# A mixture-of-experts stage with its experts ranked on the chip: fullest by twos, the others by fours

## The reference, cut to what matters

```python
p_group = softmax(t @ wg + bg); p_top_g, g_idx = top_k(p_group, 1)
e_logits = take_along_axis(einsum('td,gde->tge', t, we) + be, g_idx)[:, 0]
p_top_e, e_idx = top_k(softmax(e_logits), 2)
w_sel = p_top_g * p_top_e / sum(p_top_e)
combine = w_sel placed at (group, expert), zero elsewhere
for gi in range(4):
    hid = silu(t @ w_gate[gi]) * (t @ w_up[gi]) * combine[:, gi]     # per expert
    out = out + hid @ w_down[gi]
```

## Time and profile before

| | |
|---|---|
| profiled execution's own time | 1947.95 us |
| its span, first to last instruction | 1946.2 us |
| TensorE matmul busy | 1761.8 us (91%) |
| VectorE / ScalarE busy | 504.7 / 319.5 us |
| read from HBM | 348.36 MB, 180 GB/s over the span |
| mean granted TensorE clock | 0.942 of 2.4 GHz |

### The profile page before, as it was taken

One profiled execution on the slowest core, in us unless ns is written; L12 is line 12 of the kernel. 1 busy time (PEld: TensorE's weight loads), 2 busy tenths in 40 slices (PEclk: granted clock), 3 DMA queues, 4 the chain that ended last, 5 costly groups with the idle time before them and its releaser, 6 DMA issues.

```text
span 1946.2 us, 20288 instructions
## 1 busy us (share of the span) xinstructions
PE 1761.8 (91%) x8574; PEld 1020.0 (52%) x8574; DVE 504.7 (26%) x1222; ACT 319.5 (16%) x656; POOL 0.2 (0%) x4
## 2 busy tenths in 40 slices
PE   5899679999699999999988999997889998979797
PEld 2555578788644444444433444443664443457565
DVE  2200453412211011111014620204661013040481
ACT  2210220110200000000003200011231110031271
POOL 0000000000000000000000000000000000000000
PEclk9899866999899999999998999999899999979898
DMA  9667900323669999999981212221001111122100
GB/s 365 253 244 283 379 13 1 130 90 144 266 252 425 428 425 427 426 428 427 426 347 36 87 44 87 87 87 43 1 1 43 68 62 57 73 76 104 46 2 22
DMA packets 31953, 350.48 MB, mean 180 GB/s; under 512 B 3879, under 2 KB 10184, under 8 KB 11016
## 3 DMA queue, kind: packets, MB, share of 16 engines
q1 hardware_dynamic: 26448, 341.85, 43.3%
q10 hardware_dynamic: 5432, 7.58, 1.1%
HBM read 348.36 MB, written 1.05 MB: 180 GB/s over the span
## 4 chain that ended last, share of the span: by engine, by line
PE 81%; DVE 9%; ACT 4%; issue 2%; DMA 2%; PEld 1%; PEldq 0%; ACTq 0%; DVEq 0%; SPq 0%
PE bank L644 29%; PE bank L1310 11%; PE bank L1355 6%; PE bank L673 4%; PE bank L1300 3%; PE bank L1986 3%; PE bank L1320 3%; PE bank L661 2%; PE bank L1981 2%; PE bank L502 2%; PE bank L1074 1%; PE bank L1062 1%; PE bank L824 1%; PE bank L815 1%; PE bank L1865 1%
## 5 line engine op out<-in xcount | busy, mean ns | idle before, releaser
L644 PE MATMUL bank<-H,ring 128*128 128x512 f32 (+1 forms) x1632 | 551.8, 500 | 16.5 <-DVEq L285 8.2
L644 PEld LDWEIGHTS bank<-H,ring 128*128 128x128 f32 x1632 | 314.4, 194 | 247.7 <-issue 215.0
L1310 PE MATMUL bank<-ring,work 128*64 128x512 f32 x768 | 226.1, 593 | 0.8 <-DVE work L1397 0.8
L1310 PEld LDWEIGHTS bank<-ring,work 128*64 128x64 f32 x768 | 77.5, 137 | 142.4 <-issue 141.4
L1355 PE MATMUL bank<-work 128*64 128x512 f32 x512 | 113.4, 594 | 8.0 <-DVE work L1397 7.6
L1310 PE MATMUL bank<-work 128*64 128x512 f32 x256 | 113.2, 595 | 0.0
L673 PE MATMUL bank<-ring,H 128*128 128x512 f32 x192 | 83.6, 594 | 0.0
L1418 DVE TENSOR_TENSOR work<-work,bank 128x512 f32<-128x512 f32 x16 | 11.0, 689 | 266.0 <-PE bank L1310 266.0
L1355 PEld LDWEIGHTS bank<-work 128*64 128x64 f32 x512 | 41.9, 137 | 69.2 <-issue 57.8
L1300 PEld LDWEIGHTS bank<-work 128*128 128x128 f32 x512 | 60.2, 196 | 15.3 <-issue 12.2
L1300 PE MATMUL bank<-work 128*128 128x128 f32 x512 | 63.2, 283 | 2.9 <-DVE work L1405 2.9
(11 more groups left out here) (351 smaller groups left out, 1748.4 us busy)
## 6 DMA issues: line engine op xcount, KB each, us to landing
ring<-in_moe_w_gate SPq DMA_DIRECT2D x32, 2048.0 KB, 13.0
work<-in_moe_w_down SPq DMA_DIRECT2D x32, 2048.0 KB, 13.4
ring<-in_moe_w_up SPq DMA_DIRECT2D x16, 2048.0 KB, 11.5
work<-in_moe_w_up SPq DMA_DIRECT2D x16, 2048.0 KB, 16.0
ring<-in_ab_w_in SPq DMA_DIRECT2D x14, 2048.0 KB, 8.0
ring<-in_ada_w SPq DMA_DIRECT2D x12, 2048.0 KB, 9.7
ring<-in_w_in SPq DMA_DIRECT2D x12, 2048.0 KB, 8.2
ring<-in_w_mod SPq DMA_DIRECT2D x12, 2048.0 KB, 9.0
```

The source lines that it names most:

```text
L644: mm = nc.tensor.matmul(bank[i % NB][:, 0:n], weight(c, k, j * P, (j + 1) * P), rhs(k), start=(k == 0), stop=(k == kt - 1))
L1310: mm = nc.tensor.matmul(bank[b][rows, :], x[:, k, rows], pair_slot[i + e][:, k * 512:(k + 1) * 512], start=(k == 0), stop=(k == DT - 1), s ...
```

## The change

The router also ranks the experts by token count on the chip. After the place matmuls, VectorE forms a key for each expert (32 x count - number) in a row, TensorE transposes it, VectorE counts the greater keys (`rank`) and makes a permutation matrix (`ranked`); six small matmuls bring `place`, the combine weights, the experts' numbers (`ids`) and the keys into ranked order. The overflow test now asks whether the fullest has more than 64 tokens or the ninth more than 32.

The expert stage takes the 24 less full experts first, by fours with 32 slots each in 6 passes, and then the eight fullest by twos with 64 slots in 4 passes, all written out without run-time loops. SyncE waits for `ids_out`, reads the experts' numbers into registers, and loads half matrices of 1 MB (8 KB per partition, out of rows of 16 KB) into eight slots of 1 MB: six in the ring, two in `work`. A step is one half of gate, up or down for all experts of the pass; TensorE reports each with `step_used`, and a load waits until the step that used its slot eight pieces ago is done. Nothing is loaded for the experts before the ranking is there. Two of the three ring slots come free for the second block with the last hidden product, the third after the last down step.

```diff
-CAP = 64
+N_WIDE = 8
+CAP_WIDE, CAP_SLIM = 64, 32
+CAP = CAP_WIDE
...
-            slot_until[s] = (now[0] + i, "experts")
+            slot_until[s] = (now[0] + i, "experts" if i < 2 else "experts' last")
...
+            pe.wait_ge(lane_out, 1)
+            nc.tensor.transpose(bank[0][0:2 * NX, 0:P], key_row, ident[:])
+            for t in range(TT):
+                mm = nc.tensor.transpose(bank[1][0:2 * NX, t * P:(t + 1) * P], by_expert[:, t, :], ident[:])
+            mm.then_inc(lane_mm, 1)
+            pe.wait_ge(lane_out, 2)
+            for t in range(TT):
+                for half in range(2):
+                    rows = slice(half * NX, (half + 1) * NX)
+                    nc.tensor.matmul(bank[6 + half][:, t * NX:(t + 1) * NX], by_lane[rows, t * P:(t + 1) * P], ranked[rows, :],
+                                     start=True, stop=True, skip_group_check=True)
+            nc.tensor.matmul(bank[6][:, 4 * NX:5 * NX], bc(vec("lane")[0:NX, :], [NX, P]), ranked[0:NX, :], start=True, stop=True, skip_group_check=True)
+            nc.tensor.matmul(bank[6][:, 5 * NX:6 * NX], bc(key_col[0:NX, :], [NX, P]), ranked[0:NX, :],
+                             start=True, stop=True, skip_group_check=True).then_inc(lane_mm, 1)
...
+            L(V.tensor_tensor(by_expert[:, :, 0:NX], bank[0][:, 0:2 * NX].rearrange("p (t e) -> p t e", e=NX), member, ALU.mult))
+            L(V.tensor_copy(by_expert[:, :, NX:2 * NX], comb))
+
+            L(V.scalar_tensor_tensor(out=key_row[:, 0:NX], in0=bank[1][:, 0:NX], scalar=float(NX), in1=slot_no[:, 0:NX], op0=ALU.mult, op1=ALU.subtract))
+            V.tensor_copy(key_row[:, NX:2 * NX], key_row[:, 0:NX]).then_inc(lane_out, 1)
+            dve.wait_ge(lane_mm, 1)
+            both = slice(0, 2 * NX)
+            L(V.tensor_copy(key_col[both, :], bank[0][both, 0:1]))
+            L(V.tensor_scalar(above[both, :], key_row[both, 0:NX], key_col[both, :], None, ALU.is_gt))
+            L(V.tensor_reduce(rank[both, :], above[both, :], AXX, ALU.add))
+            L(V.tensor_copy(by_lane[both, :], bank[1][both, 0:T]))
+            V.tensor_scalar(ranked[both, :], slot_no[both, 0:NX], rank[both, :], None, ALU.is_equal).then_inc(lane_out, 1)
+            dve.wait_ge(lane_mm, 2)
+            L(V.tensor_copy(ids, bank[6][:, 4 * NX:5 * NX]))
...
+            V.tensor_tensor(over, last_col[:, 0:1], last_col[:, 1:2], ALU.max).then_inc(ids_out, 1)
+            L(V.tensor_scalar(place.rearrange("p t e -> p (t e)"), bank[6][:, 0:2 * NX], -1.0, None, ALU.add))
+            L(V.tensor_copy(comb_s.rearrange("p t e -> p (t e)"), bank[7][:, 0:2 * NX]))
...
+        PASSES = [(N_WIDE + 4 * i, 4) for i in range((NX - N_WIDE) // 4)] + [(2 * i, 2) for i in range(N_WIDE // 2)]
+        HALF = SLOT // 2
+        NHALF = 8
...
+        def half_src(w, e, half):
+
+            return w[bass.ds(e, 1), :, half * HALF:(half + 1) * HALF].rearrange("e p n -> p (e n)")
+
+        def sparse_sync(sp):
+            for p, (first, experts) in enumerate(PASSES):
+                e = [sp.value_load(ids[0:1, first + i:first + i + 1], min_val=0, max_val=NX - 1) for i in range(experts)]
+                for j, w in enumerate((wg, wu, wd)):
+                    for half in range(2):
+                        n = 6 * p + 2 * j + half
+                        for i in range(experts):
+                            at = load_at[n] + i
+                            if at >= NHALF:
+                                sp.wait_ge(step_used, step_of[at - NHALF] + 1)
+                            sp.dma_start(half_slot[at % NHALF], half_src(w, e[i], half)).then_inc(step_in[n % 4], 16)
...
         def moe_sync(sp):
-            pair_loads(sp, 0, True)
-            sp.wait_ge(stage_done, 3 * 6)
+            sp.wait_ge(ids_out, 1)
+            sp.wait_ge(stage_done, 3 * 5)
...
+            def project(p, b, n):
+
+                experts = PASSES[p][1]
+                w = P // experts
+                for half in range(2):
+                    pe.wait_ge(step_in[(n + half) % 4], filled_to[n + half])
+                    for k in range(4 * half, 4 * half + 4):
+                        for e in range(experts):
+                            rows = slice(e * w, (e + 1) * w)
+                            mm = nc.tensor.matmul(bank[b][rows, :], gath[:, k, rows], half_slot[(load_at[n + half] + e) % NHALF][:, (k % 4) * 512:(k % 4 + 1) * 512],
+                                                  start=(k == 0), stop=(k == DT - 1), skip_group_check=True)
+                    mm.then_inc(step_used, 1)
...
+            last_use["experts' last"] = (moe_ring_free, 2)
```

More of the change, by code:

```diff
@@ L1111, in build @@
         hrows = ar.take(TT, D)
-        place = ar.take(TT, NX + 2)
+        place = ar.take(TT, NX)
+        comb_s = ar.take(TT, NX)
+        ids = ar.take(NX).bitcast(I32)
         slot_no = ar.take(CAP)
@@ L1320, in scatter @@
                         mm = nc.tensor.matmul(bank[4 + 2 * t + half][:], pick_t[:, t, :], py[:, half * 512:(half + 1) * 512],
-                                              start=start, stop=stop, skip_group_check=True)
+                                              start=(p == 0), stop=(p == NPASS - 1), skip_group_check=True)
                 return mm
[L1324 to L1336, removed]
+            gather(0)
+            for p in range(NPASS):
+                pe.wait_ge(gath_out, 2 * p + 2)
+                project(p, 0, 6 * p)
+                if p:
+                    scatter(p - 1)
+                project(p, 1, 6 * p + 2)
+                if p < NPASS - 1:
+                    gather(p + 1)
                 pe.wait_ge(hid_out, p + 1)
@@ L1344, in pair @@
                 mm.then_inc(pick_mm, 1)
-                if not last:
-                    pe.wait_ge(gath_out, p * 2 + 4)
+                if p < NPASS - 1:
+                    pe.wait_ge(gath_out, 2 * p + 4)
                 pe.wait_ge(phid_t_out, p + 1)
[L1348 to L1366, removed]
+                down(p, 6 * p + 4)
+            scatter(NPASS - 1).then_inc(scat_mm, 1)
         def sparse_act(act):
-            def take_gathered(n):
-                act.wait_ge(gath_mm, n)
+            def take_gathered(p):
+                act.wait_ge(gath_mm, 2 * p + 1)
@@ L1408, in make_pick_w @@
             def make_pick_w(p):
-                for t in range(TT):
-                    for e in range(2):
-                        ins = nc.vector.tensor_scalar(pick_w[:, t, e * CAP:(e + 1) * CAP], slot_no, of(place, t, p * 2 + e),
-                                                      of(comb, t, p * 2 + e), ALU.is_equal, ALU.mult)
-                ins.then_inc(pick_w_ready, 1)
-            def pair(p, last):
-                dve.wait_ge(up_mm, p + 1)
+                o, shape, first, experts, w = slots(p, pick_w)
```

150 lines of the change are left out of this document (78 added, 72 removed).

## The result

The changed kernel takes 1977.44 us in the median of 4 runs, the kernel before 1950.68 (4 runs on the same chip): ratio 1.014, interval [1.0116, 1.0164], 27 us slower. The forecast was 1968, and the sign and most of the terms came as written, but the sum of the terms was +16.9 us and the measured change is 10 us more. The profiled execution took 1976.9 us.

The account below looks back on a forecast made before the run. The prediction took TensorE, closely followed by the 201.3 MB weight transfer, to bound the expert stage. Ranking and reads (first issue 546.8), stream (to 1025.9) and tail (8.1) gave +16.9 us, a forecast of 1968 us, range 1956 to 1993.

Parts of the forecast that it names:

- The bound: Expert stage: TensorE paces it with the DMA queue also full; with TensorE's work cut, the 201.3 MB transfer stands behind it.
- Four experts side by side: Expert projections: one over four 32-column tiles takes about 7 us, like one over two 64-column tiles (6.87).
- The chain in front: Router's end: ranking gives the identities at 543.8 us, register reads follow, first weight issue at 546.8.
- The register reads: SyncE before the first load: overflow flag, branch and four identities take 3.0 us, bounds 1.2 and 5.9.
- The stream: Expert weight loads: all 201.3 MB follow the first issue, 476 us (bounds 471 and 510) plus 3.1 around them.
- The price of 8 KB rows: Half-matrix loads: 423 GB/s, from a line through 427 with 16 KB rows and 395 with 1.7 KB packets.
- The ring starves: Rival, chance 0.10: in passes by fours eight slots hold only two steps; late returns cost 40 us, total 2008.
- The limit of 7.5 us: Passes by fours: TensorE must return a step within some 7.5 us of its landing; half clock needs 6.9 to 7.0.
- The tail: After the last landing: last down half 3.55, hand-over 0.89 and scatter 3.68, together 8.1 us, ending at 1034.0.
- No slower: Rival, chance 0.10: 426 GB/s is TensorE's demand, not the queue's limit; at 438 the sum is zero, at 448 total 1942.
- The sum: Whole stage: its end moves from 1017.14 to 1034.0 us, +16.9; +10 with the low ends, +54 with the high.
- the two slower rivals: Dearer half matrices (chance 0.14; 1984 at 410 GB/s, 2002 at 395) and the starving ring (0.10; 2008).

Follow-up runs that it names:

- e8: The changed kernel, eight slots kept, with useless matmuls filling TensorE's idle time in the passes by fours; stage 503.0 us, ratio 1.0120 to the kernel before.
- e1: The changed kernel with 14 slots of 1 MB instead of 8, nothing else; stage 501.5 us, ratio 1.0115 to the kernel before.
- e7: The kernel before with the first pair's early loads held back until the router stage ends; stage 489.8 us against 480.1, ratio 1.0053.
- e6: Changed kernel with experts 0 to 3 fixed first, 28 ranked, and seven 2 MB slots with whole matrices; stage 476.6 us, ratio 0.9993 to the kernel before.
- e5: Changed kernel with experts 0 to 3 fixed first by twos, 28 ranked, and 14 slots of 1 MB; stage 476.2 us, ratio 0.9975 to the kernel before.

## Why the prediction was right or wrong

**The bound.** Right. TensorE's work fell out of the way in the passes by fours, and the stage became the transfer of 201.3 MB plus what stands in front of and behind it.

**Four experts side by side.** Right: a half step takes 3.64 us at full clock; by twos a whole projection takes 7.09, so a half 3.55.

**The chain in front.** Right in its sum. The identities stood 5.96 us after the place product (539.91 and 0.16), 6.7 by the forecast. The register reads came to 3.3 us up to the first issue, 3.0 forecast; in the chain the flag takes 0.9 with the branch, and each identity 0.54 to 0.58 from one read to the next. First issue: 9.3 us behind the place product, 9.7 forecast. The 3.0 was a choice between bounds of 1.2 and 5.9 with no row for a single read, so its closeness is in part luck. The six small matmuls took 1.9 us where 2.7 stood.

**The stream.** Here the sum failed. From the first issue to the landing of the last piece I had 479.1 us (3.1 + 476). The last piece landed at 1034.9: 491.5 us, 12.4 too long. The price of 8 KB rows explains 2 to 3: 420 to 421 GB/s instead of 423, close to the line drawn through 16 KB and 1.7 KB. The other 9 are the rate in the passes by fours, 361 x (1 - 410/421) = 9.4 us.

**The rival that was real.** "The ring starves" was priced as all or nothing: 40 us if the clock stayed down during dense work, one to two us otherwise. The clock did come back in dense work, as expected, and 9 us were lost all the same. Two things in that step were wrong. The limit of 7.5 us for returning a step was worked out as if the queue gave its full rate until it is empty; steps returned after 5.9 to 6.4 us, inside the limit, and around 620 and 680 us the rate had already fallen to 384 to 393, with the share at 0.97 to 0.99. It is no fixed line either: between 550 and 590 us steps came back after 6.0 to 6.2 us, and the rate held at 417 to 422. And I counted the half clock as harmless because a whole step at half clock would still fit, so its only price seemed to be the one late down step. e8 shows that the late return by the clock causes the loss with this ring, and e1 that a deeper ring takes it away with the clock still low (0.81); so it takes both, a cold engine and a shallow ring.

**The tail.** Right. 1043.30 - 1034.9 = 8.4 us, 8.1 forecast.

**No slower.** Its condition, a queue that reaches 438 GB/s when asked, is refuted: 420 to 421 in e1 over 361 us with work always queued, 425 to 430 in whole 2 MB loads in e7, and 427 in e6 with TensorE idle for a third of the time. Both resources were really full at once in the kernel before.

**The sum.** +16.9 forecast, +29.1 in the stage. Step by step from e7: 9.7 for late loads with nothing else changed, 8.3 for the first issue that comes later than e7's, 17 for the slower stream (7 by 8 KB rows against 427, 9 to 10 by the ring and the clock), and 6 back by the shorter tail (8.4 instead of e7's 13.9): 29. This is an account between single profiles; of its terms the first, the rows and the ring have runs of their own. The hold-back of the loads was in the sum but never named with its own price; e7 shows that a third of the loss is there.

**The range** (1956 to 1993) held the time, and that is in part luck. The forecast's own spread was +10 to +24 us; +27 in the medians and +29 in the stage lie beyond it. The range was wide enough because it took in the near ends of the two slower rivals, neither of which came as priced: what was real lay between the "one to two us" and the 40 us of the starving ring. Within 1% was given the largest chance; the measured 1.4% lies just beyond it.

What stays open: why the rate falls before the queue is dry. Part of the loss sits where new pieces join: the one issued at 613.61 us, 3.4 us before the last piece ahead of it landed, itself landed 3.5 us behind that one instead of the usual 2.5. But the one issued at 593.27 with 3.8 us ahead lost nothing, and other late landings have no such neighbour. The runs show that the rate falls and under which conditions, not what in the path of a request makes it so.

## What to carry to other kernels

Before halving an engine's work, look whether a second resource stands at a share of 1.00 behind it; if so, the gain must come from where that one idles, here the time under the router. A change that makes addresses depend on a late result gives just that time away. Count ring depth in microseconds of transfer against the slowest release, with the waiting engine at its low clock, and leave more than the arithmetic asks. Count the size of the last step too, since all of it follows the last landing (e6). Data-dependent order can be had without the loss when a few items keep a fixed order and fill the time until the ranking is known (e5).

## What the runs showed of the hardware

The DMA share is no measure of the rate: in thin stretches it stood at 0.98 with 384 GB/s, against 1.01 with 420 in full ones. Of 1 MB pieces with 8 KB rows, queued, 421 GB/s came through; of 2 MB with 16 KB rows 425 to 430. Useless matmuls in TensorE's idle time raised the rate of the weight stream by 2% (410 to 419), since with its clock higher (0.95 instead of 0.78) TensorE gave the slots back sooner.
